# A two-part transformer kernel: the inverse rms formed on tokens by partitions at the end of a stage, and the next stage's weights split early

## The chip, the cores and the metric

One core of one Trainium2 chip. Each engine runs its own queue of instructions in order, and the queues meet only at semaphores and at the end of a block. The time is the device time of one launch in microseconds (us); lower is better.

## The reference

All arithmetic is in float32. Two blocks of two layers each, width D = 1024, FF = 2816. The first block works on 512 tokens (256 latent, 256 context) and later on 256, the second on 256. Each layer is

```python
x = x + 0.5 * swiglu(rms_norm(x) [* gain, + shift], w_in, w_out)   # half FFN "ffn1"
x = x + mixer(rms_norm(x), ...)                                    # attention and gates
x = x + 0.5 * swiglu(rms_norm(x), w_in, w_out)                     # half FFN "ffn2"

def rms_norm_2(x, g, eps=NORM_EPS):
    xf = x.astype(jnp.float32)
    y = xf * lax.rsqrt(jnp.mean(xf * xf, axis=-1, keepdims=True) + eps)
    return (y * g.astype(jnp.float32)).astype(x.dtype)
```

In the first block the gain and the shift also depend on a conditioning vector, the product of which is the first stage. A last norm follows the last layer. That makes thirteen norms over D.

## The kernel before

x lies in SBUF with the width on the partitions: 8 chunks (KD) of 128, each 512 or 256 tokens wide. A product of float32 is made of three fp32r matmuls: each factor is split in a high part (a copy in fp32r) and a low part (the rest), and `product_of_parts` (L493 to L497) adds high x high, high x low and low x high.

**Weights.** `weight_plan` lists all products in units of 128 x 2048 (an FFN's "in" unit, two DMAs of 512 KB) or 128 x 1408 ("out" unit). A ring of four slots holds them; SyncE loads the unit four ahead as soon as TensorE has raised `unit_done` for the slot's last one (`load_weights`, L319 to L333). `weight_parts` (L449) makes for a stage the three steps of a unit: ScalarE's `split_high` (L463, the copy at L472), VectorE's `split_low` (L474, the subtraction at L480) and TensorE's `wait_parts`. Two part buffers (512 tokens, mixers) or four (half FFN with 256 tokens) are used in turn; `split_high` waits for the unit that had the buffer before. The buffers are allocated anew for every stage (`scoped`, `part_buffers`), and every stage splits its own units only.

**Stages.** conditioning (nine units, "mod0"), then for layers 0 and 1: half FFN ffn1 (38 units: 11 in, 8 out, 11 in, 8 out), mixer, product with w_out (4 units, `add_product_of_parts`), half FFN ffn2; then the rope tables and the second block: ffn1_b0, mixer b0 (in_b0, attentions, merge_b0, out_b0), ffn2_b0, the same for b1, the final norm and the output. Every stage is one or more `nc.Block()`s, at the end of which the engines wait for each other. In ffn1_0 and ffn2_0 the modulation of later layers is also computed beside the products (`ModStream`), with two pairs of PSUM banks for the products instead of four.

**The end of a stage.** In the last product of a half FFN, `unit_out` of ScalarE (L995) first splits the unit `depth` ahead, if the stage has one, then waits for VectorE's add and squares that chunk of x (L390). VectorE's `unit_out` (L1094) waits for the product, adds it to x (L1101) and then makes the low part of the unit `depth` ahead. GpSimd adds up the squares of chunks 0 to 6 (L405). `add_product_of_parts` does the same for its 4 units of two chunks.

**The start of a stage.** `sum_over_chunks` (L413): two f32 matmuls with a 128 x 128 matrix of ones give the sum over D in every partition, in PSUM bank 0, for all 256 or 512 tokens. ScalarE takes the root (L967; L513 in `norm_tokens`), VectorE the reciprocal into `k.rinv` (L1053; L537), both on 128 partitions x 256 or 512. Ahead of them stand `split_high` and `split_low` of unit 0 in their queues (half FFN, mixers of the second block); `split_high` of unit 1 stands right behind the root. Then per chunk: VectorE scales x by gain and inverse (L1060; L541, L544), ScalarE copies the high part (L974, L976; L525), VectorE makes the low part (L1072, L1074; L548), and TensorE starts on the first unit as the chunks come. The parts of units 1 to 3 follow behind the eight chunks.

## Time and profile before

| | |
|---|---|
| median of 3 runs | 3957.33 us (3955.28 to 3962.86) |
| the profiled execution: time; span | 3963.74 us; 3961.7 us |
| mean granted clock of TensorE | 0.933 |
| busy, share of the span | PE 88%, PEld 75%, DVE 53%, ACT 36%, POOL 6% |
| costliest operation | L496, the matmuls of product_of_parts |
| DMA | 478.33 MB, mean 121 GB/s |

PE is TensorE's matmuls, PEld its weight loads, DVE VectorE, ACT ScalarE, POOL GpSimd, SPq SyncE's queue. Lines are those of the kernel before. Times in a timeline are us from the start of the span; a row may merge several instructions (its count is the x at the end), and its brackets name the engine's idle time before it and what ended it. The matmuls' ends are modelled.

### The profile page before, as it was taken

To read this page: it belongs to the slowest core of one execution; us is meant where nothing else is said; L and a number is where in the kernel's file an instruction comes from. 1 tells how busy PE (TensorE), PEld (TensorE's weight loads), DVE (VectorE), ACT (ScalarE), POOL (GpSimd) and SP (SyncE) were. 2 spreads that over 40 slices of the span, in tenths; PEclk is the share of its full clock that TensorE was granted. 3 is DMA by queue.
4 is the path that set the end of the run, shared out by engine and by line. 5 is a ranking of instruction groups with operands and counts; after the bars stand their busy time and mean duration, and the time that the engine had idled before them with its cause. 6 is when DMAs were issued, how large, how long until landed. Compare 5 with 4: busy or idle time off the path is not lost. (4 is left out here: it accounts for less than half of the span.)

```text
span 3961.7 us, 54085 instructions
## 1 busy us (share of the span) xinstructions
PE 3490.9 (88%) x20506; PEld 2972.5 (75%) x20506; DVE 2099.9 (53%) x2729; ACT 1412.2 (36%) x2278; POOL 229.1 (6%) x169
## 2 busy tenths in 40 slices
PE   5999896789998999898799998769899999769898
PEld 4887642468887788664699998548899999548898
DVE  5767474547677433214454655554455545554554
ACT  3323302233333322212444544243344444243443
POOL 0000100100001000200000001200000001200000
PEclk8999898889999999998899999879999999879899
DMA  6666420016665233320166565204466564104464
GB/s 200 184 180 178 110 62 31 0 59 168 186 175 157 82 96 94 101 96 0 43 175 176 150 188 155 56 0 112 141 171 180 163 188 145 53 1 126 127 185 133
DMA packets 766417, 478.33 MB, mean 121 GB/s; under 512 B 35093, under 2 KB 743173, under 8 KB 766101
## 3 DMA queue, kind: packets, MB, share of 16 engines
q1 hardware_dynamic: 755872, 473.14, 42.2%
q10 hardware_dynamic: 10356, 2.63, 0.4%
q8 instruction: 126, 2.06, 0.2%
q14 instruction: 63, 0.51, 0.0%
HBM read 474.65 MB, written 1.05 MB: 120 GB/s over the span
## 5 line engine op out<-in xcount | busy, mean ns | idle before, releaser
L496 PE MATMUL psum<-normed,weights_part 128*128 128x256 f32 (+1 forms) x11232 | 1738.4, 317 | 86.7 <-DVE normed L1074 27.3
L496 PEld LDWEIGHTS psum<-normed,weights_part 128*128 128x128 f32 x11232 | 1586.7, 192 | 227.3 <-issue 82.1
L480 DVE TENSOR_TENSOR weights_part<-weights,weights_part 128x2048 fp32r<-128x2048 f32 (+1 forms) x397 | 847.4, 2137 | 755.3 <-ACT weights_part L472 755.1
L472 ACT ACTIVATE weights_part<-weights 128x2048 fp32r<-128x2048 f32 (+1 forms) x397 | 708.4, 1787 | 761.7 <-PE psum L496 350.1
L496 PE MATMUL psum<-hidden,weights_part 128*128 128x256 f32 (+1 forms) x4224 | 680.7, 323 | 0.0
L496 PEld LDWEIGHTS psum<-hidden,weights_part 128*128 128x128 f32 x4224 | 614.5, 190 | 61.5
L1267 DVE SCALAR_TENSOR_TENSOR stage<-weights,cond,stage 128x768 f32<-128x768 f32 x294 | 281.1, 1019 | 0.0
L405 POOL TENSOR_TENSOR square<-square,rinvs 128x256 f32<-128x256 f32 (+1 forms) x39 | 57.2, 1466 | 2490.3 <-ACT rinvs L390 2488.2
L1101 DVE SCALAR_TENSOR_TENSOR x<-psum,gate,x 128x256 f32<-128x256 f32 (+1 forms) x112 | 49.6, 479 | 130.8 <-PE psum L496 130.8
L858 DVE TENSOR_REDUCE negmax<-psum 128x1 f32<-128x256 f32 (+1 forms) x128 | 66.8, 524 | 94.7 <-PE psum L2347 20.0
L987 ACT ACTIVATE rinvs<-psum 128x256 f32<-128x256 f32 (+1 forms) x88 | 39.9, 453 | 212.9 <-PE psum L496 212.8
L1524 PE MATMUL psum<-h,weights 128*128 128x512 f32 (+1 forms) x224 | 98.8, 604 | 13.3 <-PEq L506 13.3
L989 ACT ACTIVATE hidden<-rinvs 128x256 f32 (+3 forms) x88 | 43.8, 498 | 177.1 <-DVE rinvs L1084 177.1
L989 ACT ACTIVATE hidden<-roots 128x256 f32 (+3 forms) x88 | 43.8, 498 | 176.2 <-DVE roots L1084 176.2
L987 ACT ACTIVATE roots<-psum 128x256 f32<-128x256 f32 (+1 forms) x88 | 40.1, 455 | 182.4 <-PE psum L496 182.2
L1084 DVE TENSOR_TENSOR rinvs<-rinvs,psum 128x256 f32<-128x256 f32 (+1 forms) x88 | 45.4, 516 | 100.2 <-ACT rinvs L987 100.2
L1524 PEld LDWEIGHTS psum<-h,weights 128*128 128x128 f32 (+1 forms) x224 | 42.1, 189 | 70.7 <-issue 70.7
L2339 PE MATMUL psum<-heads,stage 128*128 128x256 f32 (+1 forms) x128 | 49.0, 472 | 42.2 <-POOL stage L798 42.2
L496 PE MATMUL psum<-mixed_part,weights_part 128*128 128x512 f32 (+1 forms) x384 | 71.5, 351 | 11.4 <-DVE mixed_part L597 11.4
L1086 DVE TENSOR_TENSOR hidden<-rinvs,hidden 128x256 f32 (+3 forms) x88 | 46.3, 526 | 61.1 <-ACT hidden L989 61.1
L1086 DVE TENSOR_TENSOR hidden<-roots,hidden 128x256 f32 (+3 forms) x88 | 46.3, 526 | 60.7 <-ACT hidden L989 60.7
L1084 DVE TENSOR_TENSOR roots<-roots,psum 128x256 f32<-128x256 f32 (+1 forms) x88 | 45.4, 516 | 61.7 <-ACT roots L987 61.7
(304 smaller groups left out, 3234.7 us busy)
## 6 DMA issues: line engine op xcount, KB each, us to landing
weights<-in_l_ffn_w_in SPq DMA_DIRECT2D x176, 512.0 KB, 5.1
weights<-in_ffn_w_gu SPq DMA_DIRECT2D x176, 512.0 KB, 5.0
weights<-in_l_mod_w SPq DMA_DIRECT2D x168, 384.0 KB, 3.4
weights<-in_w_in SPq DMA_DIRECT2D x34, 1024.0 KB, 5.2
weights<-in_w_gate SPq DMA_DIRECT2D x64, 512.0 KB, 4.6
weights<-in_l_ffn_w_out SPq DMA_DIRECT2D x64, 384.0 KB, 3.9
weights<-in_ffn_w_down SPq DMA_DIRECT2D x64, 384.0 KB, 4.1
weights<-in_l_ffn_w_out SPq DMA_DIRECT2D x64, 320.0 KB, 3.2
```

Of the source, the lines that this page charges most:

```text
L405: k.nc.gpsimd.tensor_tensor(total, total, buffers[n % 2], ALU.add).then_inc(summed.sem, 1)
L472: nc.scalar.activation(k.parts[part][0][:, W], k.slots[slot][:, W], ACT.Copy).then_inc(high.sem, 1)
L480: nc.vector.tensor_tensor(k.parts[part][1][:, W], k.slots[slot][:, W], k.parts[part][0][:, W].bitcast(F32), ALU.subtract).then_inc(low.sem, 1)
L496: mm = k.nc.tensor.matmul(to, left[a], right[b], start=first and n == 0, stop=last and n == len(PASSES) - 1)
L858: nc.vector.tensor_reduce(k.negmax[:, j:j + 1], S[j], AX.X, ALU.max, negate=True).then_inc(t["maxed"].sem, 1)
L987: nc.scalar.activation(row[:, T], k.psum[:, bank(spec, c), T], ACT.Silu).then_inc(t["silu_done"].sem, 1)
L989: nc.scalar.activation(one(k.hidden[0], i * RING + c, col=T), row[:, T], ACT.Copy)\
L1084: nc.vector.tensor_tensor(row, row, k.psum[:, bank(spec, c) + 1, T], ALU.mult).then_inc(t["gated"].sem, 1)
L1086: nc.vector.tensor_tensor(one(k.hidden[1], i * RING + c, col=T), row, one(k.hidden[0], i * RING + c, col=T).bitcast(F32), ALU.subtract)\
L1101: last = nc.vector.scalar_tensor_tensor(row, k.psum[:, bank(spec, c), part], gate(chunk, cond) if callable(gate) else gate, row, ALU.mult, ...
L1267: ins = k.nc.vector.scalar_tensor_tensor(total, self.buffer(n), scale, total, ALU.mult, ALU.add)
L1524: mm = nc.tensor.matmul(k.psum[0:m, 2 * slot + t, :], lhs, k.h[:, kc, :], start=kc == 0, stop=kc == KD - 1)
```

## The change

**The norm.** `sum_over_chunks` goes. A new `invert_rms` runs at the end of the stage that makes x (conditioning, `add_product_of_parts`, `half_ffn`), inside its block. It puts tokens on the partitions: the squares are the stationary side and one column of ones moves, once per 128 tokens, so the sums are 128 x 2 or 128 x 4. ScalarE takes the root and VectorE the reciprocal of these. One more matmul per 128 tokens, with the inverse broadcast as stationary side and the identity moving, spreads it over all partitions, in PSUM (`k.spread`), and the next stage scales from there. `norm_tokens` has no TensorE part any more. Conditioning loads the table of the root ahead of its squares (`prepare_sqrt`).

**The parts.** The four pairs of part buffers lie at fixed places in SBUF (`region`) for the whole program. `deal_parts` gives each unit its pair and notes which unit had it before; the count of splits runs through the whole program. So a stage can split the first units of the next one: `ahead` of them.

| from | to | units split ahead |
|---|---|---|
| conditioning | ffn1_0 | 1 |
| out product (out0, out1, out_b0, out_b1) | ffn2 | 1 |
| ffn2_0 | ffn1_1 | 1 |
| ffn2_1, ffn2_b0 | ffn1_b0, ffn1_b1 | 3 |
| ffn1_b0, ffn1_b1 | in_b0, in_b1 | 2 |
| ffn1_0, ffn1_1, ffn2_b1 | mixers, final norm | 0 |

In the queues the early splits stand where the split of the unit `depth` ahead stood before. A stage with one unit ready splits unit 1 behind its normed chunks, not behind the root. SyncE's loads are as before.

```diff
+def invert_rms(k, block, tokens, last, bank=None):
+    blocks = [(b, slice(b * P, (b + 1) * P)) for b in range(tokens // P)]
+    sums = k.psum[:, 2 * ((last + 2) % RING) + 1, 0:len(blocks)]
+    k.spread = k.psum[:, 2 * (last % RING) + 1 if bank is None else bank, 0:tokens]
+    root, inverse = k.rms[:, 0, 0:len(blocks)], k.rms[:, 1, 0:len(blocks)]
...
+    @block.tensor
+    def _(pe):
+        pe.wait_ge(summed.sem, chunks_summed)
+        pe.wait_ge(k.banks_free, RING + last)
+        for n, part in enumerate((total, buffers[(KD - 1) % 2])):
+            if n:
+                pe.wait_ge(squared.sem, chunks_squared)
+            for b, columns in blocks:
+                mm = k.nc.tensor.matmul(sums[:, b:b + 1], part[:, columns], k.const("ones")[:, 0:1],
+                                        start=(n, b) == (0, 0), stop=n == 1, skip_group_check=True)
+        mm.then_inc(t["added"].sem, 1)
+        pe.wait_ge(t["inverse"].sem, t["inverse"].base + 1)
+        for b, columns in blocks:
+            mm = k.nc.tensor.matmul(k.spread[:, columns], inverse[:, b:b + 1].broadcast_to([P, P]), k.const("ident"),
+                                    start=True, stop=True)
+        mm.then_inc(t["spread"].sem, 1)
...
+        k.nc.scalar.activation(root, sums, ACT.Sqrt, bias=k.eps[:, 0:1], scale=1.0 / D).then_inc(t["root"].sem, 1)
...
+        k.nc.vector.reciprocal(inverse, root).then_inc(t["inverse"].sem, 1)
...
+def deal_parts(k):
...
+        for c in range(spec.n):
+            u = spec.start + c
+            allowed = range(spec.parts if before is None or before >= spec.parts or c >= 2 else before)
+            part = min(allowed, key=lambda p: used.get(p, -1))
+            k.part_of[u], k.part_before[u] = part, used.get(part)
...
 # half_ffn
+    def split(half, engine, i, q):
+
+        if q < total + ahead:
+            half(k, engine, i, first + q)
...
 # half_ffn, ScalarE
-            split_high(act, 0, 0)
-
-            act.wait_ge(t["summed"].sem, t["summed"].base + 1)
-            nc.scalar.activation(k.root[:, T], k.psum[:, 0, T], ACT.Sqrt, bias=k.eps[:, 0:1], scale=1.0 / D)\
-                .then_inc(t["root_done"].sem, 1)
-            split_high(act, 0, 1)
+            for q in range(ready, 1):
+                split(split_high, act, 0, q)
             for c in range(KD):
...
-            for q in range(2, depth):
-                split_high(act, 0, q)
+            for q in range(max(ready, 1), depth):
+                split(split_high, act, 0, q)
...
                 def unit_out(i, c, spec=spec, last=s == len(specs) - 1):
-                    split_high(act, i, at(spec, c) + depth)
+                    split(split_high, act, i, at(spec, c) + depth)
                     if last:
                         act.wait_ge(k.banks_free, spec.start + c + 1 + RING)
                         square_chunk(k, act, tokens, c)
...
 # half_ffn, VectorE
-            split_low(dve, 0, 0)
-            dve.wait_ge(t["root_done"].sem, t["root_done"].base + 1)
-            nc.vector.reciprocal(k.rinv[:, T], k.root[:, T]).then_inc(t["inverse_done"].sem, 1)
-            dve.wait_ge(t["inverse_done"].sem, t["inverse_done"].base + 1)
+            for q in range(ready, 1):
+                split(split_low, dve, 0, q)
...
-                                                          k.rinv[:, part], ALU.mult, ALU.mult)
+                                                          k.spread[:, part], ALU.mult, ALU.mult)
...
                     last.then_inc(k.banks_free, 1)
-                    split_low(dve, i, at(spec, c) + depth)
+                    split(split_low, dve, i, at(spec, c) + depth)
...
+        invert_rms(k, block, tokens, first + total - 1)
...
 # conditioning, ScalarE
-            each_unit(act, 0, RING, lambda i, c: split_high(act, i, c))
-            each_unit(act, RING, spec.n, lambda i, c: split_high(act, i, c), False)
-            if l == 0:
-                for c in range(KD):
-                    square_chunk(k, act, TOK, c)
+            for c in range(spec.n + 1):
+                split_high(k, act, 0, spec.start + c)
+            prepare_sqrt(k)
+            for c in range(KD):
+                square_chunk(k, act, TOK, c)
...
 # add_product_of_parts, ScalarE (VectorE alike, ahead of its wait for the product)
-                split_high(act, 0, before + c + 2)
+                if c + 2 < spec.n:
+                    split_high(k, act, 0, spec.start + c + 2)
+                elif c + 2 - spec.n < ahead:
+                    split_high(k, act, 0, after.start + c + 2 - spec.n)
```

## Rows read from the trace of the kernel before

**Rows 1.** Page: busy shares of the engines; the costliest group with its idle time.

```profile
PE 3490.9 (88%) x20506; PEld 2972.5 (75%) x20506; DVE 2099.9 (53%) x2729; ACT 1412.2 (36%) x2278; POOL 229.1 (6%) x169
...
L496 PE MATMUL psum<-normed,weights_part 128*128 128x256 f32 (+1 forms) x11232 | 1738.4, 317 | 86.7 <-DVE normed L1074 27.3
```

**Rows 2.** Timeline (start, duration, engine, line, tiles, idle before), ffn2_b0 to ffn1_b1.

```profile
3062.72 0.42 DVE L1101 SCALAR_TENSOR_TENSOR x<-psum,x 128x256 f32<-128x256 f32 x1 [3.53 <-PE psum L496]
3063.18 0.42 ACT L390 ACTIVATE rinvs<-x 128x256 f32<-128x256 f32 x1 [3.54 <-DVE x L1101]
...
3064.16 0.67 PE L418 MATMUL psum<-square,consts 128*128 128x256 f32 x2 [1.47 <-PEq L949]
...
3068.35 1.75 DVE L1053 RECIPROCAL rinvs<-roots 128x256 f32<-128x256 f32 x1
3070.13 0.48 DVE L1060 SCALAR_TENSOR_TENSOR roots<-x,vec,rinvs 128x256 f32<-128x256 f32 x1
...
3079.48 10.61 PEld L496 LDWEIGHTS psum<-normed,weights_part 128*128 128x128 f32 x88 [0.33 <-DVE weights_part L480]
```

**Rows 3.** Timeline, out_b0 to ffn2_b0.

```profile
2861.59 0.72 POOL L405 TENSOR_TENSOR square<-square 128x256 f32<-128x256 f32 x1 [3.90 <-ACT square L390]
...
2868.63 0.48 DVE L1060 SCALAR_TENSOR_TENSOR roots<-x,vec,rinvs 128x256 f32<-128x256 f32 x1
...
2875.18 3.71 ACT L472 ACTIVATE weights_part<-weights 128x2048 fp32r<-128x2048 f32 x2
...
2877.99 7.13 PEld L496 LDWEIGHTS psum<-normed,weights_part 128*128 128x128 f32 x59 [0.28 <-DVE weights_part L480]
```

**Rows 4.** Timeline, ffn2_0 to ffn1_1, 512 tokens.

```profile
1278.67 0.63 ACT L390 ACTIVATE rinvs<-x 128x512 f32<-128x512 f32 x1 [6.85 <-DVE x L1101]
...
1283.80 3.35 DVE L1053 RECIPROCAL rinvs<-roots 128x512 f32<-128x512 f32 x1
1287.18 0.88 DVE L1060 SCALAR_TENSOR_TENSOR roots<-x,gain,rinvs 128x256 f32<-128x256 f32 x2
```

**Rows 5.** Timeline, conditioning to ffn1_0.

```profile
71.17 1.26 POOL L405 TENSOR_TENSOR square<-square 128x512 f32<-128x512 f32 x1
...
80.68 0.88 DVE L1060 SCALAR_TENSOR_TENSOR roots<-x,gain,rinvs 128x256 f32<-128x256 f32 x2
```

**Rows 6.** Timeline, ffn2_1 to the rope tables to ffn1_b0.

```profile
2170.22 0.42 ACT L390 ACTIVATE rinvs<-x 128x256 f32<-128x256 f32 x1 [3.53 <-DVE x L1101]
...
2183.42 0.48 DVE L1060 SCALAR_TENSOR_TENSOR roots<-x,vec,rinvs 128x256 f32<-128x256 f32 x1
```

**Rows 7.** SyncE's issues of one unit's two DMAs; their landing, at three times.

```profile
59.26 0.99 SPq L332 DMA_DIRECT2D weights<-in_l_ffn_w_in  x2
DMA to landing us min/median/max: 5.2/5.9/6.6
...
2165.74 1.50 SPq L332 DMA_DIRECT2D weights<-in_ffn_w_gu  x2
DMA to landing us min/median/max: 4.9/5.5/6.1
...
3058.76 0.99 SPq L332 DMA_DIRECT2D weights<-in_ffn_w_gu  x2
DMA to landing us min/median/max: 4.2/4.8/5.4
```

**Rows 8.** Page: issue-to-landing of in_w_in; timeline: first scaling of mixer b1.

```profile
weights<-in_w_in SPq DMA_DIRECT2D x34, 1024.0 KB, 5.2
...
3271.24 3.26 DVE L541 SCALAR_TENSOR_TENSOR heads<-x,vec,rinvs 128x256 f32<-128x256 f32 x8
```

**Rows 9.** Timeline: four small f32 matmuls; a table load and a one-column ACTIVATE.

```profile
752.60 0.61 PE L824 MATMUL psum<-consts,h 128*128 128x128 f32 x4
...
826.94 1.28 ACT L425 ACT_TABLE_LOAD   x1
828.24 0.20 ACT L425 ACTIVATE spare<-eps 128x1 f32<-128x1 f32 x1
```

**Rows 10.** Stretch: busy time of TensorE, granted clock, DMA share, after norm b1.

```profile
3277.60:3284.00 6.40, 6.37 (x31) 0.52 0.01 3
```

More of the change, by code:

```diff
@@ L497, in product_of_parts, with norm_tokens @@
     return mm
-def norm_tokens(k, tokens, gain, shift=None, dst=None, parts=None, splits=None):
+def norm_tokens(k, tokens, gain, shift=None, dst=None, parts=None):
     x, dst = k.x, k.h if dst is None else dst
-    mean, root, scaled, high = (k.tally(n) for n in ("mean_done", "root_done", "scaled", "normed_high"))
+    scaled, high = k.tally("scaled"), k.tally("normed_high")
     T = slice(0, tokens)
@@ L548, in _, with add_product_of_parts @@
                     k.nc.vector.tensor_tensor(parts[1][:, c, T], dst[:, c, T], parts[0][:, c, T].bitcast(F32), ALU.subtract)
-    for t, n in ((mean, 1), (root, 1), (scaled, 1 + KD), (high, KD if parts is not None else 0)):
+    for t, n in ((scaled, KD), (high, KD if parts is not None else 0)):
         t.close(n)
-def add_product_of_parts(k, spec, tokens, source, parts, gate=None, splits=None, before=0):
+def add_product_of_parts(k, spec, tokens, source, parts, gate=None, ahead=1, bank=None):
     nc, T = k.nc, slice(0, tokens)
     high, low = k.tally("source_high"), k.tally("source_low")
-    split_high, split_low, wait_parts = splits or weight_parts(k, [spec], 2)
-    ready = 0 if splits is None else 2
+    ready, after = k.ahead[spec.name], k.next_spec(spec)
+    k.ahead[after.name] = ahead
     with nc.Block() as block:
@@ L581, in _ @@
             for c in range(spec.n):
-                slot, weights = wait_parts(pe, 0, before + c)
+                slot, weights = wait_parts(k, pe, 0, spec.start + c)
                 for t in range(2):
@@ L611, in _ @@
                 last.then_inc(k.banks_free, 1)
+        invert_rms(k, block, tokens, spec.start + spec.n - 1, bank)
     high.close(KD), low.close(KD)
-    close_squares(k)
 def wide_lhs(slot, kc, t):
@@ L915, in ffn_buffers, with half_ffn @@
 def ffn_buffers(k, tokens, depth):
[L917 to L920 removed]
+    sb = region(k, PARTS_2 if depth == 2 else PARTS_4)
+    k.normed = [sb(f"normed{n}", [P, KD, tokens], F32R) for n in range(2)]
+    k.hidden = [sb(f"hidden{n}", [P, KH, tokens], F32R) for n in range(2)]
     k.rows = [k.roots[:, 1, 0:tokens], k.rinvs[:, 1, 0:tokens]]
[L922 to L925 removed]
+def half_ffn(k, tokens, name, layer, gain, shift, gate, stream=None, ahead=0):
     nc, T = k.nc, slice(0, tokens)
@@ L1076, in _ @@
                 last.then_inc(t["normed"].sem, 1)
-            for q in range(1, depth):
-                split_low(dve, 0, q)
+            for q in range(max(ready, 1), depth):
+                split(split_low, dve, 0, q)
             for s, spec in enumerate(specs):
@@ L1925, in project_heads, with split @@
     values = [k.va[:, :, 0:256], k.va[:, :, 256:512], k.bv, k.cv, k.dv]
-    split_high, split_low, wait_parts = splits
+    ready = k.ahead[spec.name]
+    def split(half, engine, c):
+        if c < spec.n:
+            half(k, engine, 0, spec.start + c)
     with nc.Block() as block:
@@ L2265, in merge_branches, with split @@
     parts = [[(0, 16, y["a"]), (3, 20, y["d"])], [(1, 16, y["b"]), (2, 18, y["c"])]]
-    split_high, split_low, wait_parts = splits
+    def split(half, engine, i, c):
+        half(k, engine, i, spec.start + c)
     def all_units(engine, unit):
@@ L2416, in second_block @@
+    sb = region(k, PARTS_2 + 27 * 1024)
+    k.merged = sb("merged", [P, KD, LAT], F32)
+    merged_parts = [sb(f"merged_part{n}", [P, KD, LAT], F32R) for n in range(2)]
+    out = k.spec(f"out_b{l}")
+    merge_branches(k, l)
+    k.ahead[out.name] = 2
+    add_product_of_parts(k, out, LAT, k.merged, merged_parts)
 def second_block(k, w):
```

347 lines of the change are left out of this document (163 added, 184 removed).

## The prediction

> **What bounds the kernel now.** I read the profile's page first (busy shares, costliest groups), then the timeline of TensorE alone to find where it stands still, then the timeline of all engines at those places. TensorE is busy 88% of the span, and the costliest group shows that the idle time before the big products was ended mostly by VectorE writing `normed` [rows 1]. So the end is set by TensorE's products plus the pauses in which all engines form one inverse rms. Thirteen such pauses exist: twelve in front of a half FFN or a mixer, one at the end. Nothing else runs on TensorE there, so what shortens the way from the last square to the first scaling (L1060, L541 or L544) shortens the kernel one for one.
>
> The pattern, at the change from ffn2_b0 to ffn1_b1 [rows 2]: the last x is added at 3062.72 for 0.42, its square runs 3063.18 to 3063.60, the block ends and the ones matmul starts at 3064.16. Behind it come the root and also both halves of the split of weight unit 0, which sit ahead of root and reciprocal on ScalarE and VectorE. The reciprocal of 128x256 starts at 3068.35 and takes 1.75, and scaling starts at 3070.13. From square to scaling: 6.53 us. With 512 tokens (ffn2_0 to ffn1_1) it runs from 1279.30 to 1287.18, 7.88 us, of which the reciprocal is 3.35 [rows 4].
>
> **The change part by part.** (1) The new chain. The sums become matmuls of one output column per 128 tokens, then a root and a reciprocal on 2 or 4 columns, then a matmul per 128 tokens that spreads the result in PSUM. Prices: four f32 matmuls of 128 columns take 0.61 [rows 9], so I take 0.6 for four and 0.4 for two, for the sums and for the spread alike (a one-column matmul is not in the trace; between 0.2 for all and the price of the wide ones, I take the upper end, as weights must still be loaded). Root: a one-column ACTIVATE takes 0.20 [rows 9], I take 0.25. Reciprocal: 1.75 for 256 and 3.35 for 512 [rows 2, 4] leave 0.15 at no columns. Hand-overs: 0.04 between add and square [rows 2], four of them. Leaving the block: 3063.60 to 3064.16 is 0.56 [rows 2]; I take 0.35, bounds 0.3 and 0.6. Sum for 256 tokens: 0.4 + 0.25 + 0.15 + 0.4 + 0.15 + 0.35 = 1.7. For 512: 0.6 + 0.25 + 0.15 + 0.6 + 0.15 + 0.4 = 2.2. Bounds for either: 1.3, and 3.5 at the slow clock.
>
> (2) One split late. Where one unit is split ahead, ScalarE's copy of unit 1 no longer goes before the normed copies but behind them, and VectorE's part waits for it. In ffn2_b0 ScalarE is free at 2875.18, so unit 1 is ready at 2875.18 + 1.9 + 2.3 = 2879.4, and TensorE, which resumed at 2877.99 [rows 3], waits 1.4 longer. At 512 tokens TensorE's first unit is longer, and I put the same effect at 1.0. It costs at six places: all norms of a half FFN but the two with three units ahead.
>
> (3) The early splits are not free everywhere. In half_ffn they stand ahead of the last squares on ScalarE and of the last adds on VectorE, and both engines take their queues in order. Unit 2 of the next stage may be loaded only when unit 6 of the last product is done. Its two DMAs, issued at 3058.76, land up to 5.4 after their issue [rows 7], about 3064.6. Then follow the copy (1.9), VectorE's part (2.3), the last add (0.42) and its square (0.42): 3069.65, six us later than now. With the new chain scaling starts at 3071.35 instead of 3070.13 [rows 2]. The stage gets back the 0.33 that TensorE waits for unit 1 at 3079.48 [rows 2]. Net 1.0 lost at ffn2_b0 to ffn1_b1. At ffn2_1 to ffn1_b0 the DMAs go at 2165.74 and land up to 6.1 later [rows 7], some 2172.5, so the last square ends at 2177.6 against 2170.64 now [rows 6]; plus 1.7, it moves the rope block that stands in between (start now about 0.6 after the square) by 8.1, while the 6.0 between rope and scaling go. Scaling comes near 2185.6 against 2183.42 [rows 6], less 0.5 for a wait: 1.7 lost.
>
> With two units ahead (ffn1_b0 and ffn1_b1 into the mixer) the last wait is for unit 1, one unit earlier. Weights of w_in land in 5.2 [rows 8], so high and low halves end about 3265.5, two adds and a square follow, and after POOL's last sum (0.7) and the chain scaling starts near 3269.0 against 3271.24 [rows 8]: 2.3 gained each instead of the 4.5 that the chain alone would give.
>
> (4) Conditioning. The early unit's DMAs go at 59.26 and land up to 6.6 later [rows 7], about 66.3. Only behind its copy and a new table load of 1.28 [rows 9] come the eight squares, which now start earlier, under the last products. POOL's adds, 1.26 and 0.17 of waiting each [rows 5], then end at 70.9 + 6 x 1.43 = 79.4 instead of 72.43 [rows 5]; eight sum matmuls and the rest at the low clock (3.9) put scaling at 83.3 against 80.68 [rows 5], plus 1.0 for (2): 3.6 lost.
>
> (5) Places with one unit ahead and no wait: in the out products POOL's last sum ends at 2862.31 [rows 3], and scaling could start 1.8 later, at 2864.1 against 2868.63: 4.5, less 1.4, is 3.1. The early split there runs between the last two units and is covered by unit 3, which takes over 6 us. If it were not, each us of it would cost one.
>
> (6) SBUF places, part numbering and semaphore counts issue no new work: nothing. The scaling now reads PSUM; VectorE's add that reads PSUM takes 0.42 against 0.48 of the scaling from SBUF [rows 2], so no cost. The final norm and the two 512-token mixer norms have no split at all.
>
> Sum, stage by stage in order of time, other places read like the one shown: ffn1_0 +3.6; mixer 0 -5.4 (7.6 becomes 2.2); ffn2_0 -3.5; ffn1_1 -4.7 (7.9 less 2.2 less 1.0); mixer 1 -4.2; ffn2_1 -3.0; ffn1_b0 +1.7; mixer b0 -2.3; ffn2_b0 -3.1; ffn1_b1 +1.0; mixer b1 -2.3; ffn2_b1 -3.1; final -2.0. Total **-27.3 us**. The profiled execution took 3963.74 (span 3961.7) and would take 3936.4; against the median of 3957.33 it is **3930.0**.
>
> On the scaling from PSUM the Trainium skill, "VectorE: DVE Perf Modes", section on the TRN2 errata, speaks against the change: it gives 120 cycles of fixed cost with a PSUM source against 58 from SBUF, at 0.96 GHz, about 0.065 us more per instruction. The rows above don't show it. By that page of the Trainium skill the sum would be some 6 to 7 us smaller.
>
> **The rivals.** A (forecast): the terms above, 3923 to 3938, chance 0.50. B: smaller gain. The chain costs a us more at every place (13 us), because small matmuls run at the low clock or leaving a block behind a matmul takes 0.6: -8 to -20, 3937 to 3949, chance 0.17. C: reading PSUM costs VectorE 0.06 more per scaling, the difference of its two rows the other way round. Seven scalings pace each of five 256-token FFN norms, fourteen halves each of three 512-token ones, eight each of three others: 101 x 0.06 = 6.1, so -21.2, 3936; chance 0.08. It is the mechanism that the Trainium skill's page above states. D: larger gain, -35 to -50, 3907 to 3922, chance 0.12. Either the early weights land before ScalarE asks (every wait of (3) and (4) gone is worth 25), which the landing rows speak against, or the shorter pauses spare TensorE the stretch at a granted clock of 0.52 after a mixer norm [rows 10], worth up to half of 6.4 at each of four mixers; still 7 to 10 us idle after the change, so I expect that stretch to stay. E: no change within 0.2%, 8 us, chance 0.08: B's surcharge at 2 us. F: slower, chance 0.05. Its mechanism is the hand-over chain itself: TensorE, ScalarE, VectorE, TensorE and the block's end now follow each other with tiny instructions. If each of the six steps cost 0.5 more than the 0.04 I read, a place would cost 3 us more, 39 in all, and the result is 12 slower, 3969. It decides from 2.7 us more per place; the 0.04 between real instructions speaks against it.
>
> **How the numbers follow.** A is the likeliest: 3930. The range leaves out F, E's upper half and D's far end: 3915 to 3947. 0.2% (8 us) is about what a measurement can tell from no change. Faster 0.87 (A to D), same 0.08, slower 0.05.
>
> **What would show it.** Reciprocals of 0.15 to 0.2 in place of 1.75 and 3.35; square to scaling 1.7 and 2.2 where nothing waits (mixer 0, mixer 1, final). In ffn2_b0 and ffn2_1 the copy of the next unit 2 ended by a DMA, ahead of the last squares, and square to square stretched by 6. In conditioning squares that start after 69. TensorE waiting 1.0 to 2.4 for unit 1 after the first unit of six half FFNs. The prediction is wrong if the last adds don't stand behind the early splits, if landing is quicker, or if the spread is slower than 0.6.

## The result, and the profile after

The changed kernel takes **3973.4 us** (median of 7 runs, 3969.8 to 3977.4) against 3957.3 of the kernel before (7 runs beside it, 3950.9 to 3962.9): ratio 1.0043, 95% interval 1.0031 to 1.0055. It is slower by 16 to 17 us, where 27 less were forecast. The profiled execution has a span of 3974.1 against 3961.7, so the rows below explain 12.4 us.

The page of the changed kernel, against [rows 1]: TensorE is busy for longer, and the costliest product waits less. The last three lines are the new spread and the new sums; 39.3 us is what TensorE waits for GpSimd ahead of them. (Groups by line and shape: busy us, mean ns | idle before, releaser.)

```profile
PE 3524.4 (89%) x20670; PEld 3014.0 (76%) x20670; DVE 2072.7 (52%) x2729; ACT 1408.2 (35%) x2278; POOL 248.1 (6%) x169
...
L535 PE MATMUL psum<-normed,weights_part 128*128 128x256 f32 (+1 forms) x11232 | 1745.0, 317 | 57.0 <-DVE weights_part L521 18.3
...
L440 PE MATMUL psum<-consts,rms 128*128 128x128 f32 x72 | 18.4, 420 | 7.2 <-DVE rms L452 7.2
L435 PE MATMUL psum<-consts,rinvs 128*128 128x1 f32 x72 | 13.3, 298 | 3.2 <-ACT rinvs L393 3.2
L435 PE MATMUL psum<-consts,square 128*128 128x1 f32 x72 | 12.5, 287 | 39.3 <-POOL square L408 39.3
```

Timeline of the changed kernel, out_b0 to ffn2_b0, which answers to [rows 3]. Nothing waits for weights here, and the chain stands bare: from GpSimd's last sum (ends 2869.83) over two passes of sums, root, reciprocal and spread to the scaling at 2872.90 are 3.07 us; 1.8 had been forecast. The late split of unit 1 then costs 1.47.

```profile
2869.11 0.72 POOL L408 TENSOR_TENSOR square<-square 128x256 f32<-128x256 f32 x1
2869.88 0.61 PE L435 MATMUL psum<-consts,square 128*128 128x1 f32 x4 [2.28 <-POOL square L408]
2870.35 0.58 PE L435 MATMUL psum<-consts,rinvs 128*128 128x1 f32 x4
2870.97 0.26 ACT L447 ACTIVATE rms<-psum,eps 128x2 f32<-128x2 f32 x1 [1.56 <-PE psum L435]
2871.27 0.17 DVE L452 RECIPROCAL rms<-rms 128x2 f32<-128x2 f32 x1 [2.87 <-ACT rms L447]
2871.49 1.07 PE L440 MATMUL psum<-consts,rms 128*128 128x128 f32 x4 [0.55 <-DVE rms L452]
2872.90 0.48 DVE L1086 SCALAR_TENSOR_TENSOR roots<-x,vec,psum 128x256 f32<-128x256 f32 x1 [1.46 <-PEq L582]
...
2883.68 1.57 PE L535 MATMUL psum<-normed,weights_part 128*128 128x256 f32 x11 [1.47 <-DVE weights_part L521]
```

The same at ffn2_b0 to ffn1_b1, which answers to [rows 2]: the last product ends at 3068.35. Of the three early splits the last is seen here: ScalarE's copy waits for the DMA, VectorE's part follows it, and the last add (ends 3074.83) and its square stand behind. TensorE is idle for 6.78 us, and its sums and its spread then take 1.01, 0.99 and 1.22 instead of 0.61, 0.58 and 1.07.

```profile
3070.26 1.91 ACT L513 ACTIVATE weights_part<-weights 128x2048 fp32r<-128x2048 f32 x1 [1.18 <-DMA weights<-in_ffn_w_gu]
3072.20 2.29 DVE L521 TENSOR_TENSOR weights_part<-weights,weights_part 128x2048 fp32r<-128x2048 f32 x1 [0.77 <-ACT weights_part L513]
3072.55 2.52 POOL L408 TENSOR_TENSOR square<-square 128x256 f32<-128x256 f32 x1 [0.86 <-ACT square L393]
3074.86 0.42 ACT L393 ACTIVATE rinvs<-x 128x256 f32<-128x256 f32 x1 [2.39 <-DVE x L1127]
3075.13 1.01 PE L435 MATMUL psum<-consts,square 128*128 128x1 f32 x4 [6.78 <-POOL square L408]
3076.00 0.99 PE L435 MATMUL psum<-consts,rinvs 128*128 128x1 f32 x4
3077.55 1.22 PE L440 MATMUL psum<-consts,rms 128*128 128x128 f32 x4 [0.55 <-DVE rms L452]
3079.10 0.48 DVE L1086 SCALAR_TENSOR_TENSOR roots<-x,vec,psum 128x256 f32<-128x256 f32 x1 [1.61 <-PEq L983]
```

Setting the starts of TensorE's products in the two profiled executions beside each other gives each place its share. The measured value is the shift at the first product after the place (the second unit of a half FFN), less the shift of the last product before the place.

| place | forecast | measured |
|---|---|---|
| conditioning to ffn1_0 | +3.6 | +5.9 |
| to mixer 0 | -5.4 | -4.4 |
| out0 to ffn2_0 | -3.5 | -0.8 |
| ffn2_0 to ffn1_1 | -4.7 | -2.6 |
| to mixer 1 | -4.2 | -2.3 |
| out1 to ffn2_1 | -3.0 | -1.2 |
| ffn2_1 to ffn1_b0 | +1.7 | +3.5 |
| to mixer b0 | -2.3 | +1.0 |
| out_b0 to ffn2_b0 | -3.1 | -1.6 |
| ffn2_b0 to ffn1_b1 | +1.0 | +4.0 |
| to mixer b1 | -2.3 | -0.9 |
| out_b1 to ffn2_b1 | -3.1 | -1.6 |
| final | -2.0 | -1.5 |
| sum | -27.3 | about -2.5 |

The other 15 us lie where the prediction changed nothing: +2.5 in mixer 0, +1.4 in mixer 1, **+2.6 and +2.8 in the two merges**, +2.1 in the input product of mixer b1, +0.6 in the two out_b products, some 2 inside the half FFNs, the rest in small pieces.

### The profile page after: what moved, and what is told of

Its sections match the earlier page's. It is cut to its first block and busy times, and to the rows that moved or that the text cites. A ratio compares the mean times of both kernels' runs of the same rounds, so it can differ in the third digit from the quotient of the medians.

```text
span 3974.1 us, 54430 instructions
## 1 busy us (share of the span) xinstructions
PE 3524.4 (89%) x20670; PEld 3014.0 (76%) x20670; DVE 2072.7 (52%) x2729; ACT 1408.2 (35%) x2278; POOL 248.1 (6%) x169
## 3 DMA queue, kind: packets, MB, share of 16 engines
HBM read 474.65 MB, written 1.05 MB: 120 GB/s over the span
## 5 line engine op out<-in xcount | busy, mean ns | idle before, releaser
L535 PEld LDWEIGHTS psum<-mixed_part,weights_part 128*128 128x128 f32 x384 | 62.9, 202 | 20.0 <-DVE weights_part L521 11.8
```

The lines of the kernel that those rows point to most:

```text
L535: mm = k.nc.tensor.matmul(to, left[a], right[b], start=first and n == 0, stop=last and n == len(PASSES) - 1)
```

## The experiments

Theory and rivals, once the result was known. **W**: early splits that wait for weights hold back the last adds and squares. **T**: the narrow chain is dearer than forecast, so it brings less. **P**: the new SBUF places slow TensorE's products. Each kernel's median stands with its ratio to the kernel before, timed beside it, and the ratio's 95% interval in brackets.

**One unit ahead.** In the changed kernel (a diff of arguments only):

```diff
-  half_ffn(..., ahead=2 if m == "ffn1" else 3 if l == 0 else 0)
+  half_ffn(..., ahead=1 if m == "ffn1" or l == 0 else 0)
-  half_ffn(k, tokens, "ffn2", l, ..., ahead=(1, 3)[l])
+  half_ffn(k, tokens, "ffn2", l, ..., ahead=1)
```

> The changed kernel with one unit split ahead instead of three (ffn2_1, ffn2_b0) and two (ffn1_b0, ffn1_b1); nothing else differs. Theory W (early splits that wait for their weights hold back the last adds and squares): in the changed kernel the last square into ffn1_b1 ends 6.9 us after the last product; without the wait it should end about 0.9 after it. Units 1 to 3 are then split late, which costs 1.4 to 2. So -4.5 at each of ffn1_b0 and ffn1_b1, -1 at each of the two mixers: 11 us shorter than the changed kernel, 3962. Rival T (the time is lost in the hand-over chain itself and in slower matmuls, and the early splits cost nothing): within 3 us of the changed kernel, 3970 to 3976. Rival L (units split late cost more than the wait): slower than the changed kernel by 4 to 8.

3952.8 us (11 runs), ratio 0.9995 [0.9986, 1.0004]: 19 to 21 less than the changed kernel, almost twice what W gave, and nothing like T or L (the rival that late splits cost more than the wait). The profile shows why W gives more than the wait. Timeline of one_ahead at the same place, last product ending at 3055.86:

```profile
3056.07 0.72 POOL L408 TENSOR_TENSOR square<-square 128x256 f32<-128x256 f32 x1
3056.36 0.42 ACT L393 ACTIVATE rinvs<-x 128x256 f32<-128x256 f32 x1 [0.91 <-DVE x L1127]
3056.85 0.61 PE L435 MATMUL psum<-consts,square 128*128 128x1 f32 x4 [0.99 <-POOL square L408]
...
3058.46 0.71 PE L440 MATMUL psum<-consts,rms 128*128 128x128 f32 x4 [0.55 <-DVE rms L452]
3059.50 0.48 DVE L1086 SCALAR_TENSOR_TENSOR roots<-x,vec,psum 128x256 f32<-128x256 f32 x1 [1.10 <-PEq L983]
```

And the granted clock over the chain (stretch, length, PE busy, PEclk, DMA share, GB/s), first of the changed kernel, then of one_ahead:

```profile
3075.00:3080.00 5.00, 3.09 (x12) 0.50 0.00 0
```

```profile
3056.50:3060.00 3.50, 1.76 (x12) 1.00 0.91 257
```

Without the 6.8 us of idle time TensorE keeps 2.4 GHz, and square to scaling falls from 3.82 to 2.72; 0.9 of these 1.1 are the second pass of sums (0.99 against 0.58) and the spread (1.22 against 0.71). GpSimd's last sum also falls from 2.52 to 0.72, since no split of VectorE runs beside it. From the first product of ffn2_b0 to that of ffn1_b1 the kernel before takes 201.5, the changed one 206.2, one_ahead 199.2; at ffn2_1 to ffn1_b0 208.1, 213.3 and 206.5. Inside ffn1_b0 and ffn1_b1 one_ahead loses 1.5 and 2.0 of it again, where TensorE waits for unit 1, which is now split late. W holds.

**No unit ahead.** One_ahead with all `ahead` at 0 (the out products behind the merges keep theirs, as in the kernel before).

> The kernel one_ahead without any early split of the next stage (the out products behind the merge keep theirs, as in the kernel before): units 0 and 1 are split at the start of their own stage, behind the chain in the queues of ScalarE and VectorE. It measures what one early unit is worth: the split (1.9 and 2.3 us) then stands between root or reciprocal and the first scaling. From the durations, scaling comes 2.5 to 4 us later at nine places before a half FFN, and in the hybrid mixers the first product waits 2 to 4 us: 25 to 35 us slower than one_ahead, 3980 to 3990. If it is less than 10 us slower, the early split was worth little even where its weights were there.

3984.3 us, ratio 1.0072 [1.0052, 1.0092], 31 more than one_ahead, as expected. One unit ahead is worth 31 us in all, the second and third cost 20: what counts is whether the weights are there when ScalarE asks, and what stands behind the split. At the conditioning even the one early unit costs: ffn1_0 has its first product at 84.39 without it and at 89.17 in one_ahead.

**The conditioning.** First all squares ahead of all splits, on the changed kernel:

```diff
+            for c in range(KD):
+                square_chunk(k, act, TOK, c)
             for c in range(spec.n + 1):
                 split_high(k, act, 0, spec.start + c)
             prepare_sqrt(k)
-            for c in range(KD):
-                square_chunk(k, act, TOK, c)
```

> The changed kernel with the eight squares of the conditioning ahead of all splits on ScalarE instead of behind the early one, and nothing else. Theory W: the squares need only x, so GpSimd's last sum no longer ends at 79.7 but before the last place of the modulation at 73; the 16 sum matmuls (3.7 us at the slow clock), root, reciprocal and spread then put the first scaling near 80 instead of 86.3: 6 us shorter, 3967. Rival T: something else (the gains, TensorE's small matmuls) ends as late as the squares, so the scaling moves by less than 2 us.

3974.2, ratio 1.0050 [1.0037, 1.0064]: no gain, an expectation missed. ScalarE waits for GpSimd between squares, so its splits and with them the whole modulation came 8 to 9 us later; the scaling stood at 87.12 against 86.28. The bound had only changed hands. The next kernel puts one square ahead of each of the last eight splits, on one_ahead:

```diff
             for c in range(spec.n + 1):
+                if c > spec.n - KD:
+                    square_chunk(k, act, TOK, c - 1 - spec.n + KD)
                 split_high(k, act, 0, spec.start + c)
```

> The kernel one_ahead with one square of the conditioning ahead of each of the last eight splits, instead of all eight behind the last (the run squares_first put all eight ahead of the first, which held ScalarE for GpSimd and shifted all splits by 8 us). ScalarE waits about 1 us for weights between two splits, and a square takes 0.61. Theory: the splits keep their times, TensorE's sums start after the last place of the modulation near 73.5 instead of 79.7, scaling near 80 instead of 86.3: 6 us shorter than one_ahead, 3947. Rival: GpSimd's sums (1.26 each) share the port with VectorE's splits and slow both down, or VectorE is the bound there: less than 3 us.

3947.9, ratio 0.9972 [0.9961, 0.9983], 5 to 9 less than one_ahead. Its timeline has the 16 sums right behind TensorE's last place, and the first scaling at 79.46, 6.8 us earlier:

```profile
72.90 1.87 PE L435 MATMUL psum<-consts,square 128*128 128x1 f32 x8
74.63 1.84 PE L435 MATMUL psum<-consts,rinvs 128*128 128x1 f32 x8
...
77.04 2.08 PE L440 MATMUL psum<-consts,rms 128*128 128x128 f32 x8 [0.57 <-DVE rms L452]
79.46 0.87 DVE L1086 SCALAR_TENSOR_TENSOR roots<-x,gain,psum 128x256 f32<-128x256 f32 x2 [2.47 <-PEq L1386]
```

**Unit 1's split.** ScalarE's half of it again ahead of the normed copies, on one_ahead (`range(ready, 1)` becomes `range(ready, 2)` ahead of the copies, `max(ready, 1)` becomes `max(ready, 2)` behind them, for ScalarE alone).

> The kernel one_ahead with ScalarE's half of unit 1's split put back ahead of the normed copies of each half FFN (VectorE's half stays behind them), which undoes step (2) of the prediction. Prediction's theory: TensorE's wait for unit 1 (1.3 to 1.5 us in the changed kernel at ffn1_0, ffn2_0, ffn1_1, ffn2_b0) falls to 0.3 or nothing, at eight half FFNs: 8 us shorter than one_ahead, 3945. Rival: ScalarE's copy (1.9 us at 256 tokens) now runs while the chain wants ScalarE or ahead of the first normed copy and pushes it back: no gain, or up to 4 us slower.

3947.4, ratio 0.9978 [0.9968, 0.9989], 5 to 7 less than one_ahead. Both sides are seen at out_b0 to ffn2_b0: the wait for unit 1 (1.50 in one_ahead) is gone, but the copy starts only when the block begins and pushes back the first normed copy, so that TensorE waits 3.18 for `normed` instead of 1.87.

```profile
2857.94 0.48 DVE L1086 SCALAR_TENSOR_TENSOR roots<-x,vec,psum 128x256 f32<-128x256 f32 x1 [1.50 <-PEq L582]
2857.96 1.91 ACT L513 ACTIVATE weights_part<-weights 128x2048 fp32r<-128x2048 f32 x1 [1.72 <-PEq L582]
...
2859.78 0.40 ACT L1004 ACTIVATE normed<-roots 128x256 fp32r<-128x256 f32 x1
...
2860.78 9.39 PE L535 MATMUL psum<-normed,weights_part 128*128 128x256 f32 x54 [3.18 <-DVE normed L1098]
```

**The old chain in the new place.** In the changed kernel `invert_rms` is written with the wide chain: two matmuls with the whole ones matrix, root and reciprocal over all tokens, `k.spread` in SBUF (`k.rinv`).

> The changed kernel with the chain of the kernel before (two matmuls with the ones matrix, root and reciprocal over all tokens, rows read from SBUF) at the place of the new one, at the end of the stage; early splits and places as in the changed kernel. The prediction's terms (1.7 us and 2.2 us for the new chain against 3.3 and 5.6 for the wide one: 0.59 or 1.02 for the second sum, 0.46 or 0.69 for the root, 1.75 or 3.35 for the reciprocal, 0.45 for hand-overs and exit) give 1.6 at each of eight 256-token places and 3.4 at each of five 512-token places: 30 us slower than the changed kernel, 4003. Theory T (small matmuls are dear: the changed kernel's trace shows 2.25 to 3.8 and 4.1 from square to scaling) gives 0.5 x 8 + 1.5 x 5: 11 to 12 us slower, 3985. If it is within 3 us the new chain is worth nothing.

The rope tables (of the second block's rotary positions), formed between ffn2_1 and ffn1_b0 in `k.rinvs`, overwrite 16 rows of the inverse in this kernel, so its values behind that place are other ones; instructions and sizes are not touched. 3982.0, ratio 1.0069 [1.0055, 1.0083]: 9 to 10 more than the changed kernel. Where one_ahead is the base:

> The kernel one_ahead with the chain of the kernel before (two ones matmuls over all tokens, root and reciprocal over 256 or 512 tokens, rows read from SBUF) at the end of the stage; the rope tables are formed in another buffer so that they leave the inverse alone (in the run wide_chain they overwrote 16 rows of it). It prices the narrow chain where no early split hides it. The prediction's terms: 1.6 at eight places and 3.4 at five: 30 us slower than one_ahead, 3983. Theory T from the traces (square to scaling 2.7 at 256 tokens and 4.2 at 512 in one_ahead, 3.3 and 5.6 for the wide chain by its terms): 0.6 x 8 + 1.4 x 5 = 12 us slower, 3965.

3969.6, ratio 1.0026 [1.0014, 1.0037], against 0.9995: 12 us by the ratios, 17 by the medians. (Other than its text says, the rope tables stayed where they were, as in wide_chain.) Last with the tables moved, on the kernel best below:

> The kernel best with the wide chain of the kernel before at the end of each stage. Here the rope tables are formed in the squares' buffer; in one_ahead_wide, other than its text says, they were not, so 16 rows of one inverse were overwritten there (instructions and sizes are the same). Theory T: the narrow chain is worth 10 to 14 us, as one_ahead_wide against one_ahead (12 by the two ratios): 3900 to 3903. The prediction's terms: 30, 3919.

3901.3, ratio 0.9861 [0.9845, 0.9877], 12.8 more than best by the medians, 8 by the ratios. Three bases give 8 to 17, near 12. Each of these differences is uncertain by some 6 to 9 us, going by the intervals of its two ratios, but none comes near 30: T holds, and the prediction's terms are more than twice too large.

**The places.** The kernel before with the hybrid mixer's buffers where the changed kernel has them (and with its 32-byte tile `rms`, which moves all later buffers alike):

```diff
-    stack, sb = scoped(k, F32)
...
+    sb = region(k, PARTS_2)
     k.normed = [sb(f"normed{n}", [P, KD, LAT], F32R) for n in range(2)]
...
+    part_buffers(k, region(k, 0, F32R), 2)
```

> The kernel before with nothing but the SBUF places of the hybrid mixer of the changed kernel (weight parts at the start of the free region, normed, values, heads, merged and its parts where the changed kernel has them). Theory P (places): in the changed kernel 24 matmuls of the merge take 3.21 us against 3.07 to 3.18, the merge 2.6 to 2.8 us more, the out product 0.3 more; the same must show here: merge 136.4 instead of 133.7, both layers together some 6 us slower than the kernel before, 3963. Rival (the matmuls are slower for what runs beside them, not for where their data lie): merge 133.7, within 1 us of the kernel before.

3966.6, ratio 1.0031 [1.0020, 1.0042]: 12 us slower. The merge (first x product to first merged_part product) lasts 131.1 and 130.7 instead of 128.5 and 128.3, as in the changed kernel (131.1 both). TensorE's timeline inside a merge, of the kernel before, of places_only, and of the changed kernel: same instructions, same clock. A group of 24 products takes 3.07 or 3.18 by turns in the kernel before, and 3.21 all along in the other two.

```profile
2708.09 3.18 PE L496 MATMUL psum<-normed,weights_part 128*128 128x256 f32 x24
...
2765.40 3.07 PE L496 MATMUL psum<-normed,weights_part 128*128 128x256 f32 x24
```

```profile
2768.78 3.21 PE L496 MATMUL psum<-normed,weights_part 128*128 128x256 f32 x24
```

```profile
2770.95 3.21 PE L535 MATMUL psum<-normed,weights_part 128*128 128x256 f32 x24
```

P holds. The rows show 5.4 of the 12 us in merges and out products and 2.2 in the input product of mixer b1, whose products start every 120.0 ns instead of every 117.8 and 113.3. Mixer 0 lasts 2.8 longer and the attentions of mixer b1 3.6 shorter in this profile, for no reason that a row shows. The two profiled executions are only 5.6 apart; the kernel before was profiled in one that took 6 us more than its median, so the rows can't show all 12. Then one_ahead with two other layouts, one in each mixer:

```diff
+    for lay in ((values, normed, heads), (heads, normed, values))[l]:
+        lay()
```

> The kernel one_ahead with other SBUF places of the hybrid mixer's buffers, weight parts staying where they are: in the first hybrid mixer values, normed, heads follow the parts (normed lies 44.0 KB behind them), in the second heads, normed, values (normed 81 KB behind). In one_ahead as in the changed kernel normed lies exactly 32 KB behind the parts, a whole number of 8 KB part buffers. Theory P1 (the product is slower when its two operands stand a whole number of buffers apart): both merges go back from 136.4 to 133.7 and both in_b products gain 1 to 2, 6 to 9 us in all, 3945. Theory P2 (it is the place of the parts themselves that is bad): no merge changes. If one layout helps and the other doesn't, it is the distance or the place of normed, and the two tell which.

3949.0, ratio 0.9983 [0.9974, 0.9992]. Merge b0 128.7, merge b1 131.1: the parts lie where they were in both, so it isn't their place; and since the slow merge b1 has `normed` 81 KB away, no whole number of 8 KB buffers, P1 fails as well. Start of `normed` less start of the parts is 44224 in b0 and 82944 in b1; what differs is the remainder by 256, 192 against 0. In the kernel before and the changed one every half FFN has 0. So small offsets were tried in single stages, first on one_ahead, then on the kernel best (below):

```diff
-    sb = region(k, PARTS_2 if depth == 2 else PARTS_4)
+    sb = region(k, (PARTS_2 if depth == 2 else PARTS_4) + pad)
```

> The kernel one_ahead with normed and hidden of each half FFN, and normed of the hybrid mixers, moved by a few bytes against the weight parts. Bytes: ffn1_0 0, ffn2_0 64, ffn1_1 192, ffn2_1 256, ffn1_b0 64, ffn2_b0 32, ffn1_b1 128, ffn2_b1 192; mixer b0 32, mixer b1 128. The merge lasts 128.5 us where the distance from parts to normed leaves 192 when divided by 512 (the kernel before, the first mixer of one_ahead_places) and 131.1 where it leaves 0 (the second mixer, one_ahead, the changed kernel). Theory R (the remainder decides): a half FFN's 1584 products take 120.4 ns each in the kernel before (remainder 0) as in the changed one; with 192 and 64 they go to 118.2, as in the input product of the kernel before: some 3.5 us less at 256 tokens; which of 32, 128 and 256 help shows how fine the rule is. Rival S (only the merge and the input product, which take their parts two by two, are touched): all half FFNs keep their 120.4.

> The kernel best with other offsets, one a stage: ffn1_0 256, ffn2_0 0, ffn1_1 64, ffn2_1 448, ffn1_b0 320, ffn2_b0 96, ffn1_b1 160, ffn2_b1 224, mixer b0 64, mixer b1 320. From first product to norm sums a half FFN of 256 tokens so far took 193 to 195 us at 0 and 256, 192 at 32, 64 and 128, 185 to 188 at 192. Theory R256 (the remainder by 256 decides): 448 gives 187, 320 gives 192, 256 in ffn1_0 leaves 390. Theory R512 (by 512): 448 and 320 differ from 192 and 64. 96, 160 and 224 fill the curve; 64 in ffn1_1 should lie between 363 and 373.

Both kernels were timed once, 3943.5 and 3915.0 us, and serve for their rows. S is refuted, since the half FFNs change too. From first product to norm sums, for a half FFN of 256 tokens, by the bytes that `normed` and `hidden` were moved (pad_map and combined have unit 1's half split early, which is worth 1 to 2 of it):

| offset | on one_ahead (pads) | on best (pad_map) |
|---|---|---|
| 0 or 256 | 194.5 to 197.5 (256: 195.1) | 192.5 to 193.9 (unit1_first) |
| 32 | 192.1 | |
| 64 or 320 | 191.7 | 190.0 |
| 96 | | 193.8 |
| 128 | 192.2 | |
| 160 | | 189.9 |
| 192 or 448 | 188.3 | 185.8 (best: 183.9 to 187.1) |
| 224 | | 190.7 |

One offset leaves up to 3 us between stages, so of the steps between offsets only those to 0, 256 and 96 on one side and 192 and 448 on the other are clear. R256 fits where it was tried: 448 does what 192 does, 256 nothing, and 320 lies with 64.

The distance between the starts of two products tells more than the stage. At 0 it is 120.0 ns in all half FFNs of 256 tokens. At 192 it is 113.3 or 117.8, and one stage can have both: ffn2_b0 of best has 117.8 in its first eleven units and 113.3 in the rest, ffn1_b0 of before_pads changes in the middle of a product. At 64 the same two values occur. So the offset sets which rates are possible, and what picks one of two is not shown. In best, at the same granted clock, 20 us hold 172 and 179 products, and in the kernel before 169 (stretch, length, PE busy and count, PEclk, DMA share, GB/s).

```profile
2840.00:2860.00 20.00, 20.00 (x172) 1.00 0.62 172
2920.00:2940.00 20.00, 20.00 (x179) 1.00 0.77 212
```

```profile
2940.00:2960.00 20.00, 20.00 (x169) 1.00 0.66 188
```

With 512 tokens the sign turns: ffn1_1 lasts 361.7 at 0 (best), 365.1 at 64 (pad_map), 372.9 at 192 (pads, 362.7 at 0 in one_ahead); 256 in ffn1_0 does nothing (388.8). TensorE's groups by shape over ffn1_b1, the kernel before and then best:

```profile
L496 PE MATMUL psum<-normed,weights_part 128*128 128x256 f32 x1056 | 129.1, 285 | 6.5 <-DVE normed L1072 6.4
L496 PE MATMUL psum<-hidden,weights_part 128*128 128x256 f32 x528 | 63.7, 283 | 0.0
```

```profile
L535 PE MATMUL psum<-normed,weights_part 128*128 128x256 f32 x1056 | 122.4, 279 | 3.2 <-DVE normed L1098 3.2
L535 PE MATMUL psum<-hidden,weights_part 128*128 128x256 f32 x528 | 60.7, 276 | 0.4 <-DVE hidden L1112 0.4
```

And over ffn1_1 with 512 tokens, at 0 (one_ahead) and at 192 (pads):

```profile
L535 PE MATMUL psum<-normed,weights_part 128*128 128x512 f32 x1056 | 242.1, 391 | 4.5 <-DVE normed L1100 3.2 <-DVE weights_part L521 1.3
```

```profile
L535 PE MATMUL psum<-normed,weights_part 128*128 128x512 f32 x1056 | 248.8, 398 | 4.4 <-DVE normed L1101 3.2 <-DVE weights_part L521 1.2
```

The same on the kernel before alone, and on the changed kernel alone:

```diff
     k.hidden = [sb(f"hidden{n}", [P, KH, tokens]) for n in range(2)]
+    if tokens == LAT:
+        sb("pad", [P, 80])
```

> The kernel before with 320 bytes between hidden and the weight parts in its five half FFNs of 256 tokens and nothing else (normed then lies 192 past a whole number of 512 from the parts; the 256-token stages of its hybrid mixers have such a distance already). Theory R2: in combined such a half FFN lasts 185 to 187 us against 193.6 to 194.0 in the kernel before; five times 6.5 to 8: 32 to 40 us less, 3920. Rival: the gain needs what else combined changes: within 3 us of the kernel before, 3955. This also tells what the changed kernel could have gained from its new places alone.

> The changed kernel with nothing but the 192 bytes in its 256-token stages (normed and hidden of five half FFNs, normed, merged and merged parts of the hybrid mixers, mixed parts of out1). Theory R2: 5.3 us back in the two merges, 2 in the out products, 6 to 9 in each of five half FFNs as in before_pads and combined: 40 to 48 us below the changed kernel's 3973, 3925 to 3933. Rival: the waits of the early splits take part of it back, since faster products leave less time for the weights to land: 3940 or more.

3919.0, ratio 0.9911 [0.9894, 0.9927], and 3919.9, ratio 0.9907 [0.9891, 0.9924]. 35 to 40 us less for the kernel before by one unused tile of 320 bytes, 53 for the changed kernel, which also gets its merges back and gains more than the 40 to 48 expected. With good places the two kernels tie: the 16 to 17 us between them are gone.

**Together.**

> All that helped, together: one unit ahead, squares of the conditioning between its splits, ScalarE's half of unit 1's split ahead of the normed copies, and normed, hidden, merged parts and mixed parts 192 bytes off a whole number of 512 behind the weight parts, in all stages. Single gains so far against the changed kernel: 20.6 for one unit ahead, 4.9 for the squares, 5.4 for unit 1, 3.8 where one of two hybrid mixers was laid out anew. Theory R: 3973 - 20.6 - 4.9 - 5.4 - 7 = 3935, less 3.5 for each of five half FFNs of 256 tokens if they gain by the remainder as the input product does (3918). Rival S: 3935. Either is 19 us or more below the kernel before (3955).

3913.3, ratio 0.9886 [0.9866, 0.9906], 5 below what R gave; ffn1_1 took 10 more, as said above. So the offset was taken back where there are 512 tokens:

> The kernel combined with the offset of 192 bytes kept where a product has 256 tokens, and taken back (0) in the three half FFNs and the out product of 512 tokens. In combined, ffn1_1 lasts 372.4 us from its first product to the sums of its norm against 362.7 in one_ahead, ffn2_0 396.8 against 394.2; in the run pads ffn1_1 with 192 lasts 372.9, ffn2_0 with 64 394.2. Theory R2 (the remainder that helps a product of 256 columns hurts one of 512): 10 less in ffn1_1, 3 in ffn2_0, up to 3 in ffn1_0: 3913 - 15 = 3898. Rival: the 10 us come from something else in these two kernels: 3913.

**3888.6 us**, ratio 0.9841 [0.9825, 0.9856], 63 to 70 us faster than the kernel before and better than expected by 9.

## Why the prediction was wrong, step by step

**Step (6), places at nothing, failed outright.** It reasoned that places issue no work. They issue none, but 24 products took 3.21 us instead of 3.07 or 3.18 [places_only]: 12 us in the medians, 7.6 of them seen in rows. No bound was set on it: the range had no term for a cost that the rows of before could not show.

**Step (1), the chain, was right in kind and too small in size, and this is the largest error.** The price of 0.4 for two matmuls was read from rows that are transposes, one instruction for each call [rows 9]. A float32 product is two: the single ones matmul of [rows 2] stands there as x2. So a pass over two blocks costs the 0.6 that the prediction gave to four. At out_b0 to ffn2_b0, term by term: sums 1.05 instead of 0.4 (two passes of two blocks, two instructions for each block: 0.61 and 0.58, overlapping), root 0.26 (0.25), reciprocal 0.17 (0.15), spread 1.07 (0.4; 0.71 where the clock stays at 2.4 GHz, here it falls to 0.50 granted on the way), exit 0.34 (0.35), hand-overs 0.04 each as read. A sum over one column costs what a transpose of 128 columns does. With 512 tokens the square ends at 1655.35 in mixer 1 and scaling starts at 1659.42: 4.07 instead of 2.2, with a spread of 2.08 at the low clock. In mixer 0 it is 3.14, at ffn1_1 4.29. At ffn2_0, where GpSimd's last sum ends behind the last square, scaling comes 6.6 behind that sum, and -3.5 became -0.8. The whole chain is worth some 12 us over the wide one in the same place, not the 30 that its terms give.

**Step (3), early splits that wait, was right on the place and short on the price.** The last square was forecast to end 6.96 behind the last product at ffn1_b1 and ended at 6.93. But the forecast carried only that delay. It left out that TensorE, idle for 7 us, comes back at half the clock (0.50 granted) and makes the chain some 0.9 longer, and that GpSimd's sums stretch from 0.72 to 2.5 beside VectorE's splits. +4.0 and +3.5 stand against +1.0 and +1.7, and the mixers b0 and b1 gave +1.0 and -0.9 instead of -2.3. All early units beyond the first cost 20 us.

**Step (2), the late split, held**: 1.27, 1.28, 1.27 and 1.47 at four half FFNs against 1.0 and 1.4. Undoing it on ScalarE gives back 5 to 7 us of the 11.0 that TensorE waits for unit 1 in the eight half FFNs of one_ahead.

**Step (4), conditioning**: GpSimd's last sum ended at 79.67 (79.4 forecast), but then came 6.6 us to the scaling (16 instructions of sums in 3.6, spread 2.08), not 3.9: +5.6 instead of +3.6.

**Step (5)** held in that nothing waits there, and lost its size to step (1): -1.6 instead of -3.1.

**The rivals.** C is refuted: VectorE's scaling from PSUM takes 0.48, as from SBUF [rows 2]. The Trainium skill, "VectorE: DVE Perf Modes", section on the TRN2 errata, has 120 cycles of fixed cost with a PSUM source against 58, an estimated 0.065 more; the rows show none of it, and they decide. F gave the right sign and time (3969) for a wrong cause: its hand-overs of 0.5 each are 0.04. B's surcharge of 1 us a place is near what happened where nothing waits (0.6 to 1.3 at 256 tokens, 0.9 to 2.1 at 512), and alone it would have given 3937 to 3949.

**The account, in the profile.** 27.3 us less were forecast and 12.4 more came, 39.7 apart. Some 25 of them lie at the thirteen places. The nine at which no more than one unit is split early missed by 15.3, 10.0 of it at the five with 512 tokens: this is nearly all the chain. The other four missed by 9.5; if the chain costs 1.3 there as at the 256-token places without a wait, some 4 are the after-effects of the waits. That makes about 20 for the chain, which fits the 18 between its 30 us of terms and the 12 measured. 15 lie outside: 5.4 in the merges, 0.6 in the out_b products and 2.3 in the input products of the hybrid mixers are the places; 3.9 in mixers 0 and 1 are not explained; the rest is small. Places_only lengthened mixer 0 by 2.8 as well; by what, was not shown. And the waits for the weights themselves, which the forecast did carry and which it put at 25 if all were gone, are worth about that: 20 by one_ahead and 5 to 9 by squares_between.

## What to carry to other kernels

Split or prefetch ahead of the last adds only what has surely landed when the engine asks: one unit ahead was worth 31 us here, the two behind it cost 20. Price a chain of tiny matmuls by the instructions that it issues (an f32 product counted twice here), at the clock that TensorE has after the wait in front of it. And when buffers move, compare one inner group of products before and after, since an SBUF address alone moved this kernel by 1%.

## What the runs showed of the hardware

- The distance of a product's two operands in SBUF sets TensorE's rate. With 256 columns, 1056 products took 129.1 us at a remainder of 0 by 256 bytes and 122.4 at 192; with 512 columns 242.1 at 0 and 248.8 at 192. The granted clock was the same (0.99). Products of 256 columns start every 120.0 ns at 0, every 113.3 or 117.8 at 192 and at 64, where the same addresses give both. The Trainium skill, "SBUF — State Buffer", section "SBUF: two separate sides", says that TensorE never waits for another engine's use of SBUF; these rows are of another kind, an address alone makes 5%, and what in SBUF or TensorE is behind it was not shown. The rule isn't whole either: the merge of the kernel before has 64 and takes 128.5, while pad_map with 64 and 320 takes 129.8 and 129.5.
- TensorE's float32 sums over 128 rows with one column moving are two instructions each. Four instructions take 0.61 at 2.4 GHz and 1.01 at 1.2 GHz, no less than four transposes of 128 columns (0.61) [rows 9].
- GpSimd's add of 128x256 takes 0.72 alone and 2.52 beside VectorE's split of 128x2048, which takes 2.29. The same page and section of the Trainium skill tells of a port pair that VectorE, with two SBUF inputs, and GpSimd lock in turn for a whole instruction. The trace agrees: the add starts 0.35 behind the split and ends 0.58 behind its end.
- The stretches at the low clock fall elsewhere from kernel to kernel: ffn1_0, with the same instructions, lasted 389.6 in one_ahead and 392.0 in the changed kernel, and twelve small matmuls in it took 1.53 and 2.82. A difference of 2.4 in one stage of one profile proves nothing.
